# Attention's projection in a two-layer decoder trunk: the last four weight chunks tile by tile, and two weight splits of the FFN made earlier

## The reference, cut to what matters

```python
for layer in range(DEPTH):                       # DEPTH = 2
    g = norm_g[layer]
    xn = _rms_norm(x, g[0])
    mix = _short_conv(...) if layer < N_A else _dilated_attention(...)   # each ends in "@ w_out" / "@ w_o"
    x = x + _rms_norm(mix, g[1])
    ff = _swiglu(_rms_norm(x, g[2]), ffn_in_w[layer], ffn_out_w[layer])
    x = x + _rms_norm(ff, g[3])
```

## Time and profile before

| | |
|---|---|
| median of three runs | 2301.97 us (2300.72 to 2304.09) |
| the profiled execution | 2302.13 us, span 2300.3 us |
| TensorE busy | 2243.9 us, 98% of the span |
| VectorE, ScalarE, GpSimd busy | 69%, 41%, 20% |
| mean granted TensorE clock | 0.995 of full speed |
| HBM | 107 GB/s over the span |

### The profile page before, as it was taken

How to read it: one execution, slowest core, us unless ns; L and a number is a source line. 1 busy time by engine, 2 the same in 40 slices (tenths; PEclk the granted TensorE clock), 3 DMA queues, 4 the chain that set the end, 5 groups by cost and what they waited for, 6 DMA issues and landing times.

```text
span 2300.3 us, 32011 instructions
## 1 busy us (share of the span) xinstructions
PE 2243.9 (98%) x10712; PEld 1869.6 (81%) x10712; DVE 1581.2 (69%) x2376; ACT 938.7 (41%) x1712; POOL 462.3 (20%) x402
## 2 busy tenths in 40 slices
PE   7999999999999999999999999999899999999998
PEld 6888887788888888877888888878788888888886
DVE  5333338877777667697666666676887777776778
ACT  4111135322223234464555655565532223223443
POOL 1000014333333201053000000001533333320113
PEclk9999999999999999999999999999999999999999
DMA  5111122333333377736333323343233333337764
GB/s 147 46 51 50 46 93 73 97 101 110 97 110 97 120 269 249 249 115 174 71 70 81 75 68 78 74 115 114 65 107 99 111 100 111 100 116 270 251 225 169
DMA packets 244852, 273.96 MB, mean 119 GB/s; under 512 B 18400, under 2 KB 157664, under 8 KB 242656
## 3 DMA queue, kind: packets, MB, share of 16 engines
q1 hardware_dynamic: 241504, 260.64, 37.2%
q10 hardware_dynamic: 3200, 11.54, 1.5%
HBM read 198.20 MB, written 48.76 MB: 107 GB/s over the span
## 4 chain that ended last, share of the span: by engine, by line
PE 87%; DVE 6%; issue 3%; ACT 2%; DMA 1%; POOL 1%; SPq 1%; DVEq 0%; POOLq 0%; ACTq 0%
PE banks L1136 35%; PE banks L1210 16%; PE banks L922 11%; PE banks L1255 9%; PE banks L1056 7%; PE banks L1292 3%; PE banks L1321 3%; PE banks L1307 3%; PE banks L969 1%; DVE down_split L2314 1%; PE banks L1335 1%; DVE xb_low L2077 1%; DVE resid L2122 0%; DVE up_split L2149 0%; ACT junk L1551 0%
## 5 line engine op out<-in xcount | busy, mean ns | idle before, releaser
L1136 PE MATMUL banks<-xb_mid,up_split 128*128 128x512 f32 x2064 | 475.9, 389 | 4.3 <-DVE up_split L2149 4.3
L1136 PEld LDWEIGHTS banks<-xb_mid,up_split 128*128 128x128 f32 x2064 | 387.1, 188 | 85.6 <-DVE up_split L2149 5.3
L1210 PE MATMUL banks<-down_split 128*128 128x512 f32 x1848 | 423.5, 390 | 4.8 <-DVE down_split L2314 3.3
L1210 PEld LDWEIGHTS banks<-down_split 128*128 128x128 f32 x1848 | 345.2, 188 | 81.8 <-DVE down_split L2314 9.0
L1136 PE MATMUL banks<-xb_low,up_split 128*128 128x512 f32 x1584 | 370.2, 392 | 4.5 <-issue 4.0
L1136 PEld LDWEIGHTS banks<-xb_low,up_split 128*128 128x128 f32 x1584 | 299.2, 189 | 68.3 <-issue 4.4
L2314 DVE TENSOR_TENSOR down_split<-down_raw,down_split 128x1024 fp32r<-128x1024 f32 x154 | 197.1, 1280 | 107.7 <-ACT down_split L1723 107.4
L1723 ACT CAST down_split<-down_raw 128x1024 fp32r<-128x1024 f32 x154 | 162.0, 1053 | 204.4 <-PE banks L1210 166.8
L2933 POOL TENSOR_TENSOR sums<-raw_up 128x512 f32<-128x512 f32 x88 | 118.3, 1348 | 481.0 <-DMA raw_up<-in_ffn_in_w 262.5
L922 PE MATMUL banks<-x_hi,w_first 128*128 128x512 f32 x768 | 184.3, 392 | 1.2 <-ACT x_hi L1490 1.1
L1255 PE MATMUL banks<-x_hi,w_second 128*128 128x512 f32 x672 | 176.4, 394 | 0.0
(11 more groups left out here) (186 smaller groups left out, 3386.5 us busy)
## 6 DMA issues: line engine op xcount, KB each, us to landing
raw_up<-in_ffn_in_w SPq DMA_DIRECT2D x88, 512.0 KB, 4.9
down_raw<-in_ffn_out_w SPq DMA_DIRECT2D x154, 256.0 KB, 3.4
down_raw<-hid_spill SPq DMA_DIRECT2D x154, 256.0 KB, 4.1
hid_spill<-hid_mix SPq DMA_DIRECT2D x110, 256.0 KB, 4.8
down_second<-in_ffn_out_w SPq DMA_DIRECT2D x66, 256.0 KB, 3.1
k_stack<-k_parts SPq DMA_DIRECT2D x32, 512.0 KB, 6.3
raw_first<-in_conv_in_w SPq DMA_DIRECT2D x24, 512.0 KB, 3.7
hid_spill<-hid SPq DMA_DIRECT2D x44, 256.0 KB, 2.0
```

The costliest lines, as they stand in the source:

```text
L1136: mm = pe.matmul(bank(b_out), up_part(ph, p, a)[:, q * P:(q + 1) * P], block(RIGHT_OF[p], b)[:, q, :], start=(i == 0), stop=(i == len(pass ...
L1210: mm = pe.matmul(bank(b_out), side[:, a, 0, i * P:(i + 1) * P], side[:, b, 1, :], start=(p in (M3, M5, M1, M2) and first and j == 0), stop ...
```

## The change

For the projection only (the first layer keeps all its orders), `token_product` goes tile by tile over chunks 12 to 15, in place of 13 to 15. The orders of ScalarE, VectorE and GpSimd in `mixer_norm` behind chunk 13's split are written anew for this phase: the casts and low parts of products 0 and 1 of the FFN's first set stand right behind chunk 15's split, those of products 2 and 3 behind tile 6; GpSimd makes the four sums of the first set's weights ahead of tile 4's means, and 10 of the 12 low parts of sums, in place of 6. The first set's weights are loaded ahead of the projection's chunk 8, in place of behind chunk 15. Slots of the weight splits are exchanged so that products 2 and 3 lie in chunk 14's place and 4 and 5 in chunk 13's. The four tables get an entry for each phase.

```diff
-UP_SLOTS = {"up0": (2, 3, 4, 5, 0, 1, 6), "up1": (4, 5, 0, 1, 2, 3, 6)}
-DOWN_SLOTS = {"down0": (1, 2, 0), "down1": (2, 0, 1)}
+UP_SLOTS = {"up0": (2, 3, 4, 5, 0, 1, 6), "up1": (4, 5, 2, 3, 0, 1, 6)}
+DOWN_SLOTS = {"down0": (1, 2, 0), "down1": (2, 1, 0)}
...
+        LOWED_POOL = {"norm1": ((5, 0), (4, 0), (5, 1), (4, 1), (5, 2), (6, 0)),
+                      "norm3": ((4, 0), (5, 0), (4, 2), (4, 1), (6, 1), (5, 2), (7, 0), (6, 0), (7, 1), (7, 2))}
+        LOWED_DVE = {"norm1": ((4, 2), (7, 0), (7, 1), (6, 2), (6, 1), (7, 2)),
+                     "norm3": ((6, 2), (5, 1))}
...
             def load_ffn(layer):
                 up = ("up0", "up1")[layer]
-                load_set(up, layer, 0)
+                if layer == 0:
+                    load_set(up, layer, 0)
                 load_set(up, layer, 1)
...
             for c in range(HT, 2 * KT):
+                if c == KT:
+                    load_set("up1", 1, 0)
                 load_row_block("oproj", o_w[0], c)
...
             def token_product(ph, norm_ph, first):
 
-                for c in range(first, 2 * KT - 3):
+                together = 4 if ph == "oproj" else 3
+                for c in range(first, 2 * KT - together):
...
                 for t in range(HT, TT):
-                    for c in range(2 * KT - 3, 2 * KT):
+                    for c in range(2 * KT - together, 2 * KT):
...
                 elif p < 2:
                     act.wait_ge(*pv_done.at("attn", STEPS * PAIRS))
+                elif p < 4:
+                    act.wait_ge(*chunk_done.at("oproj", 2 * KT - 1))
                 elif p < 6:
-                    act.wait_ge(*chunk_done.at("oproj", 2 * KT - 3 + p // 2))
+                    act.wait_ge(*chunk_done.at("oproj", 2 * KT - 2))
...
                 if n == 0:
-                    pool.wait_ge(*chunk_done.at("conv_out" if layer == 0 else "oproj", 2 * KT - 3))
+                    pool.wait_ge(*(chunk_done.at("oproj", KT - 1) if layer else chunk_done.at("conv_out", 2 * KT - 3)))
```

More of the change, by code:

```diff
@@ L1620, in mixer_norm @@
                 b22_high(norm_ph, 3)
+                if ph == "oproj":
+                    prepare(chunk0[ph] + 14)
+                    t3_high(norm_ph, 2)
+                    first_square(ph, 4)
+                    prepare(chunk0[ph] + 15)
+                    up_high(up, 0)
+                    up_high(up, 1)
+                    first_square(ph, 5)
+                    output_square(norm_ph, 4)
+                    first_square(ph, 6)
+                    first_square(ph, 7)
+                    t3_high(norm_ph, 3)
+                    second_square(norm_ph, 4)
+                    output_square(norm_ph, 5)
+                    second_square(norm_ph, 5)
+                    output_square(norm_ph, 6)
+                    up_high(up, 2)
+                    up_high(up, 3)
+                    output_square(norm_ph, 7)
+                    lower_high(norm_ph, 4)
+                    second_square(norm_ph, 6)
+                    second_square(norm_ph, 7)
+                    lower_high(norm_ph, 5)
+                    sums_high(norm_ph, 4, 0)
+                    up_high(up, 4)
+                    sums_high(norm_ph, 4, 2)
+                    sums_high(norm_ph, 5, 0)
+                    sums_high(norm_ph, 5, 1)
+                    lower_high(norm_ph, 6)
+                    sums_high(norm_ph, 4, 1)
+                    sums_high(norm_ph, 6, 1)
+                    lower_high(norm_ph, 7)
+                    sums_high(norm_ph, 5, 2)
+                    up_high(up, 5)
+                    sums_high(norm_ph, 7, 0)
+                    sums_high(norm_ph, 6, 0)
+                    sums_high(norm_ph, 6, 2)
+                    sums_high(norm_ph, 7, 1)
+                    sums_high(norm_ph, 7, 2)
+                    up_high(up, 6)
+                    return
                 first_square(ph, 4)
@@ L2066, in lower_sum @@
                 else:
-                    dve.wait_ge(*tc_done.at(ph, summed_at(t, 1)))
+                    dve.wait_ge(*tc_done.at(ph, summed_at(ph, t, 1)))
                     if t > HT:
@@ L2196, in mixer_norm @@
                 b22_low(norm_ph, 3)
+                if ph == "oproj":
+                    prepare(chunk0[ph] + 14)
+                    take_output(ph, 0, 4)
+                    take_output(ph, 0, 5)
+                    prepare(chunk0[ph] + 15)
+                    up_low(up, 0)
+                    up_low(up, 1)
+                    take_output(ph, 1, 4)
+                    whole_added(norm_ph, 4)
+                    take_output(ph, 0, 6)
+                    take_output(ph, 0, 7)
+                    normed(norm_ph, 4)
+                    take_output(ph, 1, 5)
+                    whole_added(norm_ph, 5)
+                    t3_low(norm_ph, 2)
+                    t3_low(norm_ph, 3)
+                    normed(norm_ph, 5)
+                    take_output(ph, 1, 6)
+                    whole_added(norm_ph, 6)
+                    up_low(up, 2)
+                    up_low(up, 3)
+                    take_output(ph, 1, 7)
+                    whole_added(norm_ph, 7)
+                    lower_sum(norm_ph, 4, 1)
+                    lower_sum(norm_ph, 4, 0)
+                    normed(norm_ph, 6)
+                    lower_sum(norm_ph, 5, 0)
+                    lower_sum(norm_ph, 4, 2)
+                    lower_sum(norm_ph, 5, 1)
+                    normed(norm_ph, 7)
+                    lower_low(norm_ph, 4)
+                    lower_sum(norm_ph, 6, 1)
+                    lower_low(norm_ph, 5)
+                    lower_sum(norm_ph, 5, 2)
+                    lower_sum(norm_ph, 7, 0)
+                    lower_low(norm_ph, 6)
+                    lower_low(norm_ph, 7)
+                    lower_sum(norm_ph, 6, 0)
+                    up_low(up, 4)
+                    lower_sum(norm_ph, 6, 2)
+                    lower_sum(norm_ph, 7, 1)
+                    up_low(up, 5)
+                    sums_low(norm_ph, 6, 2)
+                    lower_sum(norm_ph, 7, 2)
+                    sums_low(norm_ph, 5, 1)
+                    up_low(up, 6)
+                    return
                 prepare(chunk0[ph] + 14)
```

62 lines of the change are left out of this document (45 added, 17 removed).

## The result

The changed kernel takes 2305.81 us (median of 12 runs, 2303.87 to 2308.47); the kernel before takes 2301.97 (12 runs, 2300.67 to 2304.09). The ratio is 1.0019, with a 95% interval of 1.001 to 1.0027: slower by 3.84 us by the medians, where 3.9 was forecast, and by 2.3 to 6.2 us by the interval. The profiled execution took 2305.37 us (span 2303.6).

A forecast was written before the change was run, and what follows sets the result against it. TensorE was taken to bound the kernel (98% busy), VectorE the junction. 4.8 lost early, 6.0 won, 3.4 lost late give +2.2; with 1.7 for the clock +3.9, 2305.9 us, 8 in 10 from 2300.3 to 2309.0.

The forecast's parts named there:

- P8: Start of the second set's product 1, the moment followed through the change: from 1679.87 to 1682.05 us, +2.2.
- the prediction's own signs against it: Wrong if turn 4 is under 3 us late, P8 has no wait, or the clock drops twice or not at all.
- Early waits: Before turn 4: contention with weight sums, loads and the place of chunk 15's split make TensorE 4.8 us late.
- Junction: Turn 4 to the second set's product 0: less VectorE work behind tile 7, 27.3 us instead of 33.31.
- for fewer drains: Turn 4 to the second set's product 0: some 0.2 us less for TensorE.
- GpSimd behind the low parts: Before P8: ten lower parts delay the second set's four weight sums, so TensorE waits 3.4 us.
- The port wait of 1.07: Behind the second set's sums: a weight split held 1.07 us as the third set's first sum lands.
- P8 without the clock: P8 moves +2.2 us: 4.8 lost before turn 4, 6.0 won up to set two, 3.4 lost there.
- The clock: Behind the two longer waits, 2.7 and 3.4 us: one stretch at the lower clock, 1.7 us, bounds 0 and 3.4.
- first rival: Clock losses behind both long waits and a little more contention: +5.6 us, 2307.6; chance 0.35.
- The second rival: Before turn 4, sums don't hold VectorE and loads land early: order alone costs 2.9, no clock loss, 2302.3; chance 0.15.
- Faster: VectorE behind tile 7 no longer holds TensorE: -3.5 to -5.4 us, 2298.5 to 2296.6, if early loss under 3.7; chance 0.08.

The follow-up runs named there:

- the first experiment: The changed kernel with chunk 15's low part on VectorE ahead of the output of tile 5, not behind it: 2302.92 us, ratio 1.0001 to the kernel before.
- the low part moved: The changed kernel with the last low part (tile 7, third sum) on VectorE instead of GpSimd: 2301.94 us, ratio 0.9998 to the kernel before.
- split 15 and the low part in their places: The changed kernel, chunk 15's low part ahead of tile 5's output, last low part on VectorE: 2300.16 us; with tile 5's square earlier, first weight sums later: 2299.07.
- the fastest version: The changed kernel, chunk 15's low part and tile 5's square earlier, first weight sums later, last low part on VectorE: 2299.07 us, ratio 0.9987 to the kernel before.
- four, one wait mended: The kernel before with chunks 12 to 15 tile by tile and GpSimd's first-set weight sums waiting for chunk 6, not 12: 2303.66 us, ratio 1.0007.
- the versions with four and with three together: The fastest version, with four chunks tile by tile (2299.07 us, ratio 0.9987), and the same with only three (2299.29 us, ratio 0.9985).
- the one with the earlier norm: The fastest version with the norm of tile 6 on VectorE ahead of lower sums (4,1) and (4,0): 2299.46 us, ratio 0.9986 to the kernel before.

## Why the prediction was right

The waits, their places and what ended them were those forecast, and the total came within 0.1 us by the medians. That closeness is luck: the length to P8 came out 0.5 us below its forecast and the clock some 0.4 above, and the interval alone spans 4 us. One of the prediction's own signs against it did appear: in the profiled execution the clock dropped twice.

- **Early waits.** Forecast 0.67, 0.65, 0.8 and 2.7, in sum 4.8, as delays of TensorE's starts. TensorE stood idle for 0.27, 0.52, 0.47 and 2.27, in sum 3.5; but its starts came 0.41, 0.76, 0.72 and 2.58 late, in sum 4.5, so each wait also cost 0.14 to 0.31 us in the passes around it. Turn 4 came 35.19 us after turn 2, not 29.00: 6.2 later, the 4.5 and 1.7 for a stretch at half clock. The contention was near its price per operation (0.6 and 1.1 for 0.87 and 1.07), 2.8 in sum for 3.0. That the order alone makes most of chunk 15's wait is shown by the first experiment. That turn 4 is at 1648.49, where 1648.6 was forecast, is chance: this profile reaches turn 2 already 1.54 us earlier, and has the 1.7 behind it.
- **Junction.** Forecast 27.3 us from turn 4 to the second set, measured 26.77. The waits forecast at 0.9, 0.4, 0.7 and 0.4 came at 1.14, 0.36, 0.66 and 0.42, in sum 2.58 for 2.4. TensorE's own work there was 24.19 us, forecast 25.1 less 0.2 "for fewer drains": no row had that 0.2, and with four waits fewer it came out at 0.9, which agrees with the 0.14 to 0.31 per wait above.
- **GpSimd behind the low parts.** The sums were to end 28.4 us after turn 4 and ended 28.1 after; P8 was to start 33.45 after and did at 33.20, its wait 3.55 for 3.4. The port wait of 1.07 that the prediction had in this term is there: 5.12 us from the sums to P8, where other versions have 4.04. That GpSimd's queue and this meeting set the wait is shown by the low part moved, where both shrink.
- **P8 without the clock.** Forecast +2.2 (4.8 - 6.0 + 3.4); measured 68.39 - 65.03 - 1.7 = +1.7 (4.5 - 6.5 + 3.7).
- **The clock.** This term was mis-sized: forecast 1.7 for one stretch at half clock, and the profiled execution had two, behind both waits, which is its first rival's case. P8 came 3.4 us later after turn 2 and what follows another 1.5, in sum 4.9 there. Its span grew by only 3.3, since the profile before had one such stretch at 289 us of the span which this one lacks, and reached turn 2 1.5 us later for it. The medians differ by 3.84, which less 1.7 leaves 2.1 for the clock: more than one stretch and less than two over the 12 runs. How many each of the other runs had, and whether its splits met the third set's sum, is not in their records, so this share is worked out and not shown.
- **The second rival** (no contention, 2302.3) failed: the sums did hold VectorE. But it named the order alone as 2.85, and with the order undone the median is 2.9 lower, at 2302.92, no slower than before. The two figures agree by chance: to P8 this version is 4.45 us shorter, 1.7 for the order's own wait, 1.7 for the clock behind it and 1.0 for the pair of splits before P8.
- **Faster** failed for the reason given: ten low parts and four sums kept GpSimd from 1654.90 to 1676.57, with gaps of under 1 us. Nor does it hold once the early loss is under 3.7 us, as the prediction had it: with split 15 and the low part in their places that loss is 2.4, yet from turn 4 to P8 it takes 31.11 us, where the rival had 27.8. The kernel is then faster than before, at 2300.16 and 2299.07, but not at the rival's 2298.5 or less.

The headline edit itself, four chunks for three, is worth nothing that these runs can tell in the fastest version and loses 2.6 in the change. What lets the junction shrink is the new orders: 29.25 us from turn 4 to the second set with three chunks together, where four chunks with the old orders still take 33.19; with both it is 26.77, but the other 2.5 are paid for ahead of turn 4 and before P8. How much of it is the weight work made earlier and how much GpSimd's share of the low parts, no run separates.

## What to carry to other kernels

Work that is moved off the critical engine's queue comes back where the receiving engine's own next delivery is due: look up what stands behind it there before counting the gain. In a list of orders, an operation that must be in time for TensorE stands ahead of any that waits for a third engine. When a loop is turned from chunk by chunk to tile by tile, every wait elsewhere on "chunk c is done" has moved, and the engines queued behind those waits with it.

## What the runs showed of the chip

Over all profiles 15 waits of TensorE of 1.98 to 4.41 us lay in this region. Behind 13 of them the granted clock was half for 3.4 us (6.8 behind the longest), a loss of 1.5 to 1.7 for each 3.4; behind two, of 2.61 (one low part moved) and 2.02 us (four, one wait mended), it was not, while 1.98 had one. Waits of 1.46, 1.65 and 1.70 had none. Where a later wait for another engine followed, the loss cost nothing: the versions with four and with three together had it behind turn 6 and reached P8 in 62.61 and 62.55 us, the one with the earlier norm had none and took 62.72. I had counted such a loss as a fixed price. Behind turn 6 it was free: it fell on product 1, and the version without it waited 1.70 us before turn 7 instead, where the two with it had no wait. It was not free ahead of turn 4: there the change lost its 1.7 us although P8 waits for VectorE later, because the chain that ends in P8's wait begins with TensorE's last pass over tile 7 and moves with it (28.08 us from turn 4 to the end of the sums with the stretch, 28.12 without). Where it is not free it can make single executions differ by up to 1.7 us, which is nearly half of what was measured here.
